# Four light experts of a hybrid trunk: float32 products by two 64-column operands side by side in place of packed high and low parts

## What is computed

```python
D_FF_EXPERT = 3584

def swiglu(x, wg, wu, wd):
    return (jax.nn.silu(x @ wg) * (x @ wu)) @ wd

def moe_swiglu(x, w_router, we_gate, we_up, we_down):
    logits = (x @ w_router).astype(jnp.float32)
    top_vals, top_idx = lax.top_k(logits, TOP_K)
    gates = jax.nn.softmax(top_vals, axis=-1)
    combine = jnp.einsum("bske,bsk->bse", jax.nn.one_hot(top_idx, N_EXPERTS, dtype=jnp.float32), gates)
    out = jnp.zeros_like(x)
    for e in range(N_EXPERTS):
        out = out + combine[..., e:e + 1] * swiglu(x, we_gate[e], we_up[e], we_down[e])
    return out
```

## Time and profile before

| | |
|---|---|
| median of 3 executions | 1278.1 us (1277.04 to 1278.29) |
| span of the profiled execution, first to last instruction | 1276.0 us |
| difference between that span and the median | 2.1 us |
| PE busy | 96% of the span |
| DVE busy, ACT busy | 87%, 73% |
| data moved | 434.49 MB |

### The profile page before, as it was taken

How to read it: one execution, slowest core, us unless ns; L and a number is a source line. 1 busy time by engine, 2 the same in 40 slices (tenths; PEclk the granted TensorE clock), 3 DMA queues, 4 the chain that set the end, 5 groups by cost and what they waited for, 6 DMA issues and landing times.

```text
span 1276.0 us, 15815 instructions
## 1 busy us (share of the span) xinstructions
PE 1227.3 (96%) x6181; PEld 1053.5 (83%) x6181; DVE 1106.1 (87%) x861; ACT 933.7 (73%) x716; POOL 39.8 (3%) x57
## 2 busy tenths in 40 slices
PE   9999999999999999999999999999999999999886
PEld 8988888888989888888887877888787888887664
DVE  6978555568889999999999999999999899999887
ACT  5575444445868787888888888887988888788774
POOL 0100000001010000000000000000000000000100
PEclk9999999999999999999999999999999999999998
DMA  9947555537459999999999999999999999999993
GB/s 317 346 163 262 190 182 192 198 110 254 159 171 348 370 410 399 398 412 411 409 409 401 411 409 412 411 394 408 411 410 410 412 405 408 411 411 404 412 411 159
DMA packets 143556, 434.49 MB, mean 341 GB/s; under 512 B 8964, under 2 KB 50996, under 8 KB 131188
## 3 DMA queue, kind: packets, MB, share of 16 engines
q1 hardware_dynamic: 139936, 421.07, 85.8%
q0 software_dynamic: 3456, 12.32, 2.8%
q10 hardware_dynamic: 84, 0.02, 0.0%
HBM read 428.40 MB, written 4.98 MB: 340 GB/s over the span
## 4 chain that ended last, share of the span: by engine, by line
PE 61%; DVE 17%; DMA 15%; ACT 5%; issue 2%; SPq 0%; ACTq 0%; DVEq 0%
DVE w_lo L1032 14%; DMA raw<-in_we_down 8%; PE turn L1686 7%; PE turn L1688 7%; PE turn L1687 7%; PE accp L1686 5%; PE accp L1687 5%; PE accp L1688 5%; DMA raw<-in_we_gate 5%; PE turn L1798 4%; PE turn L1795 4%; ACT w_hi L669 4%; PE turn L1797 2%; PE turn L1796 2%; DMA raw<-in_we_up 2%
## 5 line engine op out<-in xcount | busy, mean ns | idle before, releaser
L1032 DVE TENSOR_TENSOR w_lo<-raw,w_hi 128x1792 fp32r<-128x1792 f32 (+3 forms) x447 | 895.8, 2039 | 96.8 <-ACT w_hi L669 91.5
L669 ACT CAST w_hi<-raw 128x1792 fp32r<-128x1792 f32 (+2 forms) x441 | 756.0, 1724 | 173.9 <-PE turn L1688 43.2
L2130 PE MATMUL turn<-w_hi,t_both 128*128 128x448 f32 x512 | 193.8, 379 | 16.0 <-DVE w_lo L1032 15.4
L2131 PE MATMUL turn<-w_lo,t_both 128*128 128x448 f32 x512 | 188.7, 369 | 0.0
L1686 PE MATMUL turn<-w_hi,a_hi 128*128 128x448 f32 x496 | 184.0, 371 | 0.0
L1688 PE MATMUL turn<-w_hi,a_lo 128*128 128x448 f32 x496 | 181.7, 366 | 0.0
L1687 PE MATMUL turn<-w_lo,a_hi 128*128 128x448 f32 x496 | 181.7, 366 | 0.0
L2130 PEld LDWEIGHTS turn<-w_hi,t_both 128*128 128x128 f32 x512 | 97.5, 190 | 36.6 <-issue 20.0
L2131 PEld LDWEIGHTS turn<-w_lo,t_both 128*128 128x128 f32 x512 | 97.4, 190 | 7.9 <-issue 0.2
L1686 PEld LDWEIGHTS turn<-w_hi,a_hi 128*128 128x128 f32 x496 | 93.1, 188 | 9.8
L1687 PEld LDWEIGHTS turn<-w_lo,a_hi 128*128 128x128 f32 x496 | 93.2, 188 | 8.4
(11 more groups left out here) (298 smaller groups left out, 1529.8 us busy)
## 6 DMA issues: line engine op xcount, KB each, us to landing
raw<-in_we_gate SPq DMA_DIRECT2D x128, 896.0 KB, 8.6
raw<-in_we_up SPq DMA_DIRECT2D x128, 896.0 KB, 9.2
raw<-in_we_down SPq DMA_DIRECT2D x96, 1024.0 KB, 9.6
raw<-in_w_in SPq DMA_DIRECT2D x18, 1024.0 KB, 9.0
raw<-in_we_down SPq DMA_DIRECT2D x32, 512.0 KB, 8.6
raw<-in_w_down SPq DMA_DIRECT2D x11, 1024.0 KB, 5.1
raw<-in_w_gate SPq DMA_DIRECT2D x10, 1024.0 KB, 5.3
raw<-in_w_up SPq DMA_DIRECT2D x10, 1024.0 KB, 5.4
```

The lines of the kernel that those rows point to most:

```text
L669: nc.scalar.copy(w_hi[:, p % PARTS, 0:filled(p)], raw[:, p % RING, 0:filled(p)]).then_inc(hi_done, 1)
L1032: return nc.vector.tensor_tensor(out, whole, hi.bitcast(f32), ALU.subtract)
L2130: nc.tensor.matmul(to[:, c, :], few, wh[:, kk, c, :], start=(k == 0), stop=False)
L2131: last = nc.tensor.matmul(to[:, c, :], few, wl[:, kk, c, :], start=False, stop=(k == KD - 1))
```

## The change

The light experts lose the split. Their weights are never rounded by ACT or DVE; PE multiplies `raw` as float32. The stationary operand is the 64 token columns alone (`x_few`, `hT_few`, plain float32). Two such products are put side by side in the array: one writes partitions 0 to 63 and one 64 to 127 of the same bank (`HALVES`), with two different halves of the inner columns (gate, up) or of the output columns (down). So a light unit now covers 1792 inner columns, there are 2 units to a light expert, and the light sum is one bank (`few_sum`). `raise_low`, `few_low`, the folding of two halves of the sum, and the split of the last sum are gone. A light gate or up piece is now 128 rows by 1792 columns (7168 bytes in a run, 0.918 MB as before). There are 24 units, ordered `"HHH" + "LHH" * 6 + "H" + "LL"`, and the number of pieces and bytes stays the same.

```diff
-    ORDER = "HHH" + "LH" * 12 + "H" + "L" * QUARTERS
+    ORDER = "HHH" + "LHH" * 6 + "H" + "LL"
+    UNITS_OF = {"H": 4, "L": 2}
+    ROWS_PIECES = {"H": 4, "L": 8}
...
     def mixed(i):
-        return "uuuu" if i == 0 else "uuuudddd" if i == N_UNITS - 1 else "uduududd" if light(i) else "uduuuddd"
+        if i == 0:
+            return "uuuu"
+        if i == N_UNITS - 1:
+            return "uuduuduudduuddd" + "d"
+        if light(i):
+            return "uduuduuduuud" if not light(i - 1) else "uduududuuduuddd" + "d"
+        return "uduuuddd" if not light(i - 1) else "uduuuddddddd"
...
-    WHOLE = {PLACE[piece] for piece in (("down", N_UNITS - 3, 1), ("down", N_UNITS - 2, 2))}
+    WHOLE = {PLACE[piece] for piece in PLACE if light(piece[1])}
...
-                    nc.scalar.copy(xg_few[k % 2][:, :, 0:FEW],
-                                   tokens_bank[:, 0:KD * FEW].rearrange("p (k t) -> p k t", t=FEW)).then_inc(xg_rounded, 1)
+                    nc.scalar.copy(x_few[:, k % 2, :, :],
+                                   tokens_bank[:, 0:KD * FEW].rearrange("p (k t) -> p k t", t=FEW)).then_inc(xg_done, 1)
...
-            def add_low(i, which):
-
-                to = (few_gate, few_up)[which]
-                pe.wait_ge(few_kept, 2 * number(i) - 1 + which)
-                for c in range(2):
-                    last = nc.tensor.matmul(to[:, c, :], raise_low[:], few_low[:, c * PART:(c + 1) * PART],
-                                            start=False, stop=True, skip_group_check=True)
-                last.then_inc(few_added, 1)
...
+            def few_down(i, pair):
 
                 _, s = expert_step(i)
+                half, quarter = divmod(pair, 4)
                 w = unsplit(down_piece(i, pair)).rearrange("p (j d) -> p j d", d=D)
+                hT = (hT_last if i == N_UNITS - 1 else hT_few[:]).rearrange("p (b h t) -> p b h t", h=2, t=FEW)
+                for j, block in enumerate(blocks_of(quarter)):
+                    for rows, cols in zip(HALVES, LAST):
+                        last = nc.tensor.matmul(few_sum[rows, :], hT[:, block, half, :], w[:, j, cols],
+                                                start=(s == 0 and pair == 0 and block == 0),
+                                                stop=(s == 1 and pair == 7 and block == BLOCKS - 1))
                 last.then_inc(piece_used, 1)
...
+            def few_rows(i, which, k):
...
+                w = unsplit((up_piece if which else gate_piece)(i, k)).rearrange("p (h c f) -> p h c f", h=2, c=2)
+                for c in range(2):
+                    for h, rows in enumerate(HALVES):
+                        last = nc.tensor.matmul(to[rows, c, :], x_few[:, e % 2, k, :], w[:, h, c, :],
                                                 start=(k == 0), stop=(k == KD - 1))
                 last.then_inc(piece_used, 1)
...
             def last_scatter():
 
                 pe.wait_ge(slots_read, 1)
-                pe.wait_ge(last_ys, 1)
+                pe.wait_ge(last_kept, 1)
                 for n in range(NT):
...
+                    for rows, cols in zip(HALVES, LAST):
+                        nc.tensor.matmul(last_bank(n, cols), pickT[rows, 1, n * P:(n + 1) * P].bitcast(f32),
+                                         last_rows_in[rows, :], start=True, stop=True).then_inc(scattered, 1)
```

More of the change, by code:

```diff
@@ L154, in filled @@
         which, _, pair = IN_ORDER[p - MOE_AT]
-        return len(blocks_of(pair)) * D if which == "down" else 2 * WIDE
+        return len(blocks_of(pair % 4)) * D if which == "down" else 2 * WIDE
     ctx = ExitStack()
@@ L2046, in half_step @@
                 return last
-            def few_down_pair(pair, w, first, last_one):
-                wh, wl = [a[:, 0:len(blocks_of(pair)) * D].rearrange("p (j d) -> p j d", d=D) for a in w]
-                for j, block in enumerate(blocks_of(pair)):
-                    for c in range(2):
-                        cols = slice(c * BANK, (c + 1) * BANK)
-                        nc.tensor.matmul(accp[:, 2 + c, :], hT_packed[:, block, :], wh[:, j, cols],
-                                         start=(first and block == 0), stop=False)
-                        last = nc.tensor.matmul(accp[:, 2 + c, :], hT_packed[:, block, :], wl[:, j, cols], start=False,
-                                                stop=(last_one and block == BLOCKS - 1))
-                return last
@@ L2166, in last_scatter @@
+                    if s == 0 and e:
+                        pe.wait_ge(ys_kept, KEPT.index((kind, e - 1)) + 1)
+                if light(i):
+                    few_down(i, pair)
+                else:
+                    down_pair(pair, split(down_piece(i, pair)), s == 0, s == 3).then_inc(piece_used, 1)
             def last_scatter():
                 pe.wait_ge(slots_read, 1)
-                pe.wait_ge(last_ys, 1)
+                pe.wait_ge(last_kept, 1)
                 for n in range(NT):
-                    for part in (ys_hi, ys_lo):
-                        last = nc.tensor.matmul(last_bank(n, LAST[0]), pickT[:, 1, n * P:(n + 1) * P], part[:, LAST[0]],
-                                                start=(part is ys_hi), stop=(part is ys_lo))
-                    last.then_inc(scattered, 1)
@@ L2283, in _ @@
                     before_gate(i)
-                    for pair in range(4):
+                    for pair in range(ROWS_PIECES[ORDER[i]]):
                         if pair == 1:
@@ L2296, in _ @@
                     else:
[L2297 removed]
+                        if pairs[c] == 6 and i == N_UNITS - 1:
                             turn_h(i)
@@ L2300, in _ @@
                     pairs[c] += 1
-                    if light(i) and place == 1:
-                        add_low(i, 0)
-                    if light(i) and place == kinds.rindex("u") + 1:
-                        add_low(i, 1)
-            last_down()
+            for pair in range(8):
+                down(N_UNITS - 1, pair)
             last_scatter()
```

316 lines of the change are left out of this document (109 added, 207 removed).

## The result

| | before | changed |
|---|---|---|
| median | 1277.65 us (1277.04 to 1278.29) | 1310.62 us (1306.1 to 1314.29) |
| span of the profiled execution | 1276.0 us | 1312.5 us |
| mean granted clock | 0.994 | 0.97 |

The ratio is 1.0257, with an interval of 1.0232 to 1.0282. The changed kernel is 33 us slower, where the forecast had it 15.5 us faster, and the time lies 48 us above the forecast and far outside the range.

The account below looks back on a forecast made before the run. The prediction took DMA transfers as the bound after 460 us, PE in the first three heavy units, and a serial tail in the last 22 us. 1276.0 - 11 (transfers) - 6.5 (tail) + 2 (slots) = 1260.5 us span, median 1262.6, range 1254 to 1281.

Parts of the forecast that it names:

- the one on the slots: Light pieces hold slots until PE has used them; three slots stay in flight, 2 us added, bounds 0 and 6.
- The third rival: Transfers gain nothing from longer runs and slots are held at every light unit: 1268 to 1281 us, chance 0.10.
- The array: Light unit's products on PE: halves taken as overlapping, 36.4 us against 72.7 without; up to 47.7 before PE bounds.
- The rivals of no and of partial overlap: Array halves in light units: no overlap, about 1442 us, chance 0.11; partial, 1282 to 1400 us, chance 0.08.
- ACT and DVE: Half the expert pieces no longer split, some 330 us of DVE's work, hidden behind transfers: costed at nothing.
- The transfers: Light gate and up weights come in runs of 7168 bytes for 3584: 11 us less, bounds 0 and 13.
- The tail: After the last landing: no splits, one block left for PE, earlier scatter; 6.5 us less, bounds 5 and 8.5.
- The clock: PE partly at 1.2 GHz in light units; slots hide it except at the very end, up to 1.5 us.
- The sum: Whole kernel: 1276.0 - 11 - 6.5 + 2 = 1260.5 us span, median 1262.6 us.

Follow-up runs that it names:

- The one-sided kernel: Changed kernel with eight slots, all light products in the lower array half for six of each eight gate and up and six of eight down pieces: 1409.3 us.
- the run with long runs: Kernel before, with only the light experts' gate and up loads changed to runs of 7168 bytes: 1271.15 us, ratio 0.9943.
- fillers: Changed kernel with 16 extra float32r products at two places of each cycle to keep PE busy: 1309.88 us, ratio 1.0243.
- the seven-slot kernel: Changed kernel with one more slot in the ring (7 in place of 6) from the ninth expert piece on: 1274.21 us, ratio 0.9975.
- the eight-slot one: Changed kernel with two more slots in the ring (8 in place of 6) from the ninth expert piece on: 1262.46 us, ratio 0.9879.

## Why the prediction was wrong

**The step that failed is the one on the slots.** It ran: the pieces ahead go through ACT and DVE, some 4 us, after HH another 1.9 us, "6 us are under three pieces of 2.2 us, so three slots stay in flight", 2 us added, bounds 0 and 6. Measured, the slots cost 48 us (1310.62 against 1262.46 with eight). Two things in it were wrong.

The lag was taken as some 4 us through ACT and DVE and 1.9 us of PE, when it is the time until PE reaches the piece: the first light piece lies landed for nearly 11 us, five pieces and not under three. The 4 us were right, and in place of the 1.9 us stand 6.8 us for three pieces that are split and wait ahead of PE. PE takes 2.4 us for a heavy piece (28.9 us for a unit of 12), so four full parts are 9.6 us; that bound was to be had before the run. The 1.9 us themselves were too small: split products of 448 columns start 0.203 us apart and those of 512 columns 0.231, so a heavy unit is 96 x 0.203 + 42 x 0.231 + 0.8 = 30.0 us and falls 3.0 us behind the transfers. With six slots, five held pieces leave one in flight, where 7.4 us from issue to landing at 2.2 us a piece are over three.

And the bound of 6 us was read from the first 60 us of HHH, where DVE frees the slots. It measures what PE's slowness costs when the ring doesn't wait for PE. The late release is another mechanism, and the run with it alone (+40 us in the old order, at a granted clock of 0.995) shows that it isn't a single loss at the start: it goes on through the middle, at 390 GB/s for 408.

The third rival, "slots are held at every light unit", named the mechanism rightly and carried the same cap of 6 us, so it ended at 1281 instead of 1311; its other half, that longer runs gain nothing, is refuted. With its price unbounded it would have been the case of the other side that the prediction lacked; its chance of 0.10 was too small besides.

**The array.** Right, and at the favourable end: full overlap, 0.19 us an instruction. The estimate from the Trainium skill, page "TensorE: Matmul & The Clock Gate", Part 3 (1.59 times for two tiles) is too low for this case, whose trace shows 2.0. The rivals of no and of partial overlap are refuted. The one-sided kernel shows what they would have looked like, and that my working was too low for them: six pieces of eight without overlap make the light unit about 64 us in place of 72.7, so 1442 becomes some 1370 us, and it took 1409. The trace assigns most of those 40 us: 16 heavy units of 30.0 us in place of 28.9 are 18 us, and about 50 changes into light products and out again at 0.3 to 0.35 us are 15 to 17 us. So the switches between 64 and 128 columns, set at nothing, do have a price, within the bound of 0.2 us each; in the kernels that the transfers bound it is hidden.

**ACT and DVE.** Right. DVE's share fell to 55% with nothing gained from it by itself.

**The transfers.** Right in kind, too large in size: 11 us predicted, 6.5 and 8.4 measured. The estimate from the Trainium skill, page "DMA: Bandwidth & Descriptors", section on small descriptors, was 3.8 us; the measurement lies between the two. The packets in the trace of the run with long runs did get shorter as the line said: the 16384 of 7168 bytes take 280 ns on average, where twice as many of 3584 bytes took 146 ns each, 13 us less over 16 engines. Why only half of that reached the time wasn't found.

**The tail.** 5.2 us measured for 6.5. The windows around the last landing answer to the earlier trace rows:

```profile
1292.00:1294.00 2.00, 1.45 (x8) 0.34 (x6) 0.00 (x0) 0.00 (x0) 0.00 (x0) 1.00 1.03 426
1294.00:1296.00 2.00, 1.57 (x8) 0.29 (x4) 0.00 (x0) 0.00 (x0) 0.00 (x0) 1.00 0.62 242
```

242 of some 420 GB/s fill 1.2 of the last 2 us, so the last landing counts as 1295.2 us, and the span ends 17.3 us behind it. Before, by the same reckoning, gives 1253.5 and 22.5 us. The end in order of time:

```profile
1296.10 2.80 PE L2000 MATMUL accp<-raw,y_work 128*64 128x512 f32 x12 [0.53 <-DMA raw<-in_we_down]
1298.94 0.59 ACT L947 COPY more_rows<-accp 128x512 f32<-128x512 f32 x1 [18.91 <-PE accp L2000]
1299.67 1.99 PE L2083 MATMUL turn<-more_rows,pickT 64*128 64x512 f32 x8 [0.78 <-ACT more_rows L947]
```

PE waited for the DMA until 1296.1 and then had three blocks (12 instructions) to do, not one. The scatter gave back a part: I had four products at 0.86 us, 3.4 us, and its eight instructions took 1.99.

**The clock.** The predicted dips came (0.97 overall). With fillers the clock rose and the time didn't change, so they are not the cause of the loss; what they cost by themselves isn't separated from what the fillers take.

**The sum.** With eight slots the kernel takes 1262.5 us, and the forecast was 1262.6. That is partly luck, since errors cancel: the transfers gave 2.6 to 4.5 us less and the tail about 1 us less (16.9 us in this kernel by the same reckoning, so 5.6 for 6.5), while the 2 us for slots fell away and the two extra slots let the transfers run ahead, 367 GB/s from 370 to 480 us for 360, another 1.9 us. But it says where the error was: the forecast held for a kernel whose ring covers PE's lag.

**What stays open.** Why PE doesn't work off its lag within a light unit, where it needs less for a piece than the 2.2 us of the transfers, in the kernel where only the release is late (there, eight split products at 0.2 us, 1.6 us a piece); I only argue that each refilled slot arrives late by the same amount. Also the spread of the seven-slot kernel, 1270 to 1279.

**The best version** is the eight-slot one, 1262.46 us: 1.2% under the kernel before and 3.7% under the changed one. It holds for this input: the path for an expert with more than 128 tokens, which is not taken here, would no longer be right in it.

## What to carry to other kernels

When a change moves a buffer's release from a fast early consumer to the last one, count in pieces how far the last one runs behind the landing, every full buffer between them included, add the pieces in flight, and compare with the ring: here five and over three against six slots cost 48 us, and with eight the rate was back. The count fits these runs and is argued, not tested on another kernel; how few pieces in flight would do isn't shown, since the 7.4 us were themselves taken with about three in flight. Take a stall's bound from a stretch with the same releaser, or measure the release alone, which is an edit of two lines. And where the DMA is the bound, look at GB/s and not at busy digits: 385 and 408 both read as 9.

## What the runs showed of the hardware

Two float32 products of 64 columns in different halves of the array overlapped completely, 0.19 us an instruction of 448 columns against 0.375 in one half, also when the four instructions of one half stood ahead of the four of the other. Going from split products of 128 columns to these and back cost some 0.35 us. Products that use different halves of the rows were fast too: eight instructions of the scatter (64 rows, 512 columns) took 1.99 us, 0.25 us each with the last one's tail, where one with all rows takes 0.43; no run has them all in one half, so that this is overlap isn't shown. And longer runs than 3584 bytes still pay: 7168 bytes gave 411 against 408 GB/s with nothing else changed.
